# The first block of a two-block transformer layer, turned to token-major like the second

## What is computed

```python
h = rms_norm(x, norm_mix[l])
proj = jnp.einsum('btd,dn->btn', h, w_in[l])
q_a, f_a, i_a, g_a, q_b, k_b, v_b, gate_logits = jnp.split(proj, split_pts, axis=-1)
gates = jax.nn.sigmoid((gate_logits + b_gate[l]).astype(jnp.float32)).astype(x.dtype)
gate_a, gate_b = jnp.split(gates, 2, axis=-1)

y_a = hgrn2_mixer(q_a, f_a, i_a, g_a, lower_bounds[l], hgrn_out_gain[l])
y_b = chunked_relpos_attention(q_b, k_b, v_b, q_gain[l], k_gain[l], rel_bias[l])

merged = (gate_a * jnp.einsum('btc,cd->btd', y_a, w_proj_a[l])
          + gate_b * jnp.einsum('btc,cd->btd', y_b, w_proj_b[l]))
x = x + jnp.einsum('btd,de->bte', merged, w_out[l])
```

## Time and profile before

| | |
|---|---|
| median of 3 runs | 2746.28 us (2742.32 to 2750.71) |
| the profiled execution | 2749.1 us, its span 2747.2 us, so 1.9 us lie around the span |
| granted TensorE clock, mean | 0.986 |
| busy: PE matmuls, PE weight loads, DVE, ACT | 97%, 84%, 65%, 45% |
| chain of work that ended last | PE 90%, DVE 4%, DMA 2%, ACT 2% |
| first matmul of group 0 starts | 22.27 us |
| group 15 starts, proj_b ends | about 398 us, about 704 us |

### The profile page before, as it was taken

How to read it: one execution, slowest core, us unless ns; L and a number is a source line. 1 busy time by engine, 2 the same in 40 slices (tenths; PEclk the granted TensorE clock), 3 DMA queues, 4 the chain that set the end, 5 groups by cost and what they waited for, 6 DMA issues and landing times.

```text
span 2747.2 us, 39546 instructions
## 1 busy us (share of the span) xinstructions
PE 2666.8 (97%) x14450; PEld 2318.1 (84%) x14450; DVE 1782.5 (65%) x2072; ACT 1223.1 (45%) x1456; POOL 11.6 (0%) x15
## 2 busy tenths in 40 slices
PE   6999999999999999999999899999879999999998
PEld 6999999999887888888888788887768888888886
DVE  6766653545776777777777676885666565656565
ACT  4444444454454444444444544455444443444343
POOL 0000000000000000000000000000000000000000
PEclk9999998999999999999999999999989999999999
DMA  6865554455788777777777577773646666666663
GB/s 215 262 209 165 154 169 122 150 190 182 241 268 259 251 252 251 248 250 250 253 250 247 156 231 217 214 222 132 209 136 228 209 209 220 208 212 209 209 217 133
DMA packets 304408, 577.52 MB, mean 210 GB/s; under 512 B 17584, under 2 KB 27968, under 8 KB 304016
## 3 DMA queue, kind: packets, MB, share of 16 engines
q1 hardware_dynamic: 303392, 571.58, 65.6%
q0 software_dynamic: 880, 4.02, 0.5%
HBM read 573.42 MB, written 2.11 MB: 209 GB/s over the span
## 4 chain that ended last, share of the span: by engine, by line
PE 90%; DVE 4%; DMA 2%; ACT 2%; issue 2%; SPq 0%; DVEq 0%; ACTq 0%
PE acc L1086 82%; PE W L1086 6%; DMA raw<-in_w_out 1%; PE W L1149 1%; DVE wlo L1525 1%; DMA raw<-in_w_ffn_in 1%; DVE adaacc L1547 1%; ACT whi L510 1%; ACT arena L546 0%; PE W L1255 0%; DVE hL L1586 0%; PE acc L1375 0%; DMA arena<-in_xT 0%; DVE arena L1622 0%; DVE arena L2119 0%
## 5 line engine op out<-in xcount | busy, mean ns | idle before, releaser
L1525 DVE TENSOR_TENSOR wlo<-raw,whi 128x1024 fp32r<-128x1024 f32 x888 | 1080.9, 1224 | 803.6 <-ACT whi L510 800.9
L510 ACT ACTIVATE whi<-raw 128x1024 fp32r<-128x1024 f32 x888 | 935.2, 1059 | 1218.8 <-PE acc L1086 1013.0
L1086 PE MATMUL acc<-whi,hH 128*128 128x512 f32 x1952 | 533.8, 395 | 9.3 <-issue 6.4
L1086 PE MATMUL acc<-whi,hL 128*128 128x512 f32 x1952 | 523.4, 390 | 0.0
L1086 PE MATMUL acc<-wlo,hH 128*128 128x512 f32 x1952 | 522.8, 390 | 0.0
L1086 PEld LDWEIGHTS acc<-whi,hL 128*128 128x128 f32 x1952 | 367.0, 188 | 77.9
L1086 PEld LDWEIGHTS acc<-wlo,hH 128*128 128x128 f32 x1952 | 366.9, 188 | 77.2
L1086 PEld LDWEIGHTS acc<-whi,hH 128*128 128x128 f32 x1952 | 361.9, 189 | 81.1 <-issue 10.6
L1547 DVE SCALAR_TENSOR_TENSOR adaacc<-raw,cs,adaacc 128x512 f32<-128x512 f32 x360 | 269.8, 749 | 8.7 <-DMA raw<-in_w_ada 1.9
L1086 PE MATMUL acc<-whi,yH 128*128 128x512 f32 x864 | 235.6, 395 | 4.8 <-issue 4.8
L1086 PE MATMUL acc<-wlo,yH 128*128 128x512 f32 x864 | 232.1, 391 | 0.0
(11 more groups left out here) (197 smaller groups left out, 1465.3 us busy)
## 6 DMA issues: line engine op xcount, KB each, us to landing
raw<-in_w_in SPq DMA_DIRECT2D x264, 512.0 KB, 4.4
raw<-in_w_ada SPq DMA_DIRECT2D x192, 512.0 KB, 4.7
raw<-in_w_ffn_in SPq DMA_DIRECT2D x176, 512.0 KB, 4.6
raw<-in_w_up SPq DMA_DIRECT2D x128, 512.0 KB, 4.5
raw<-in_w_down SPq DMA_DIRECT2D x128, 512.0 KB, 4.2
raw<-in_w_ffn_out SPq DMA_DIRECT2D x88, 512.0 KB, 4.7
raw<-in_w_out SPq DMA_DIRECT2D x32, 512.0 KB, 4.8
raw<-in_w_o SPq DMA_DIRECT2D x32, 512.0 KB, 4.5
```

What stands on the lines that cost most here:

```text
L510: act.activation(whi[:, v], raw[:, s], ACT.Copy).then_inc(S("w_hi"), 1)
L1086: return pe.matmul(o, l, r, start=start, stop=stop, skip_group_check=True)
L1525: dve.tensor_tensor(wlo[:, v], raw[:, s], whi[:, v].bitcast(F32), ALU.subtract)\
```

## The change

Mode A is gone. All groups of the first block run in mode B, so results have tokens on partitions, and:

- **First norm.** `hH` and `hL` are made from x times the gain alone (`x_low` on DVE). x is loaded a second time by rows; ACT squares it with a running sum behind group 0 (`first_norm`), and rstd, now one number per partition, is a scale of each evacuation (`evac_sig`, `evac_copy`, `silu`, `gate_lin`).
- **f and q** are turned on PE after evacuation (`fq_turn`, 8 transposes each, four times) into the half of `acc` they came from.
- **Head norms**: DVE sums along the free dimension (`head_reduce`), multiplies by the reciprocal roots there, and PE turns the result (`head_turn`, 16 transposes each, three times). `head_sum` and `head_spread` are gone.
- **Gate bias** is a row now: loaded broadcast by the GpSimd queue (`gate_bias`, 8 loads of 256 KB), added on DVE (`gate_lin`), then ACT's sigmoid in place.
- **Merged activations** are turned (`turn_merged`, 8 transposes, four times) before they are split.

```diff
+            sp.dma_start(col[:], A["cols"]).then_inc(S("cols_in"), 16)
+            x_chunk(0)
+            first(0)
+            first(1)
...
+            first(5)
             sp.dma_start(cst[:], A["consts"]).then_inc(S("tables_in"), 16)
+            sp.dma_start(xn0, A["x"].rearrange("(t p) n -> p t n", p=P)).then_inc(S("x_rows"), 16)
+            first(6)
+            first(7)
...
+            for u in range(8):
+                if u % 2 == 0:
+                    act.wait_ge(S(f"x_in{u // 2}"), 16)
+                for j in (2 * u, 2 * u + 1):
+                    ins = act.activation(hH[:, j], x0[:, j], ACT.Identity, scale=V("norm_mix", 1, j))
+                ins.then_inc(S("x_hi"), 1)
                 hi()
...
+                act.wait_ge(S("x_rows"), 16)
+                for t in range(TT):
+                    act.activation(blk(6 + t), xn0[:, t], ACT.Square, accum_out=tot[:, t:t + 1]).then_inc(S("x_sq"), 1)
...
+            group(hooks={2: off_copy, 4: gate_sig(0, M), 5: head_square(0), 7: head_root(0)})
+            group(hooks={0: head_square(1), 1: head_root(1), 2: ya_hi, 3: head_square(2), 4: gate_sig(1, M),
+                         5: head_root(2), 6: head_copy(1)})
+            group(hooks={2: head_copy(2), 4: gate_sig(2, M)})
...
-                            for m in range({"A": GT, "B": 0}[mode]):
-                                ins = mm(a[:, m * T:(m + 1) * T], wt[:, m * P:(m + 1) * P], x[:, kt],
-                                         first and m % 2 == 0, last)
-                            for t in range({"A": 0, "B": TT}[mode]):
+                            for t in range(TT):
                                 ins = mm(a[:, t * GCOL:(t + 1) * GCOL], x[:, kt, t * P:(t + 1) * P], wt, first, last)
...
+            group(8, hH, hL, (), hooks={2: fq_turn(0)})
             pl.phase("q_i")
+            group(8, hH, hL, (("f_in", 1),), hooks={2: fq_turn(1)})
+            group(8, hH, hL, (("f_in", 2),), hooks={3: fq_turn(2)})
+            group(8, hH, hL, (("q_in", 1),), hooks={3: fq_turn(3)})
...
+            group(8, hH, hL, (("vb_in", 2),), hooks={1: hgrn_out, 6: head_turn(0)})
+            group(8, hH, hL, (("gate_lin", 1),), hooks={3: head_turn(1), 6: head_turn(2)})
+            group(8, hH, hL, (("gate_lin", 2),), hooks={7: slot(0, 0, N_B)})
...
+            group(hooks={3: gate_lin(0, M), 6: head_reduce(0), 7: head_apply(0)})
+            group(hooks={1: head_reduce(1), 2: ya_low, 3: gate_lin(1, M), 4: also(head_apply(1), head_reduce(2)),
+                         7: head_apply(2)})
+            group(hooks={3: gate_lin(2, M)})
...
+                hooks = {3: lambda: turn_x1(i - 1)} if i else {1: turn_merged(3)}
```

More of the change, by code:

```diff
@@ L484, in _ @@
             pool.wait_ge(S("ext_out"), 16)
-            pool.wait_ge(S("hn_done"), 1)
+            gate_bias(0)
+            gate_bias(1)
+            for n in (2, 3):
+                pool.wait_ge(S("gate_lin"), n - 1)
+                gate_bias(n)
+            pool.wait_ge(S("hn_in"), 1)
             src = bass.AP(scratch.tensor, 0, [[1, P], [EXT, H], [1, T]])
             pool.dma_start(tiles(HK), src).then_inc(S("hk_in"), 16)
+            for n in range(4, 8):
+                pool.wait_ge(S("gate_lin"), n - 1)
+                gate_bias(n)
             pool.wait_ge(S("att_s"), N_B)
@@ L701, in _, with head_copy @@
-            group(hooks={2: head_root(2), 3: gate_sig(16, 136, mg(2), 8)})
+                act.wait_ge(S("hn_turn"), 1)
+                for h in range(H):
+                    ins = act.activation(yH[:, h], Wf[:, h * T:(h + 1) * T], ACT.Identity, scale=V("out_gain", 1, h))
+                ins.then_inc(S("y_hi"), 1)
+            def head_copy(k):
+                def run():
+                    x, g = ((qb, q_scale[:]), (kb, V("k_gain")))[k - 1]
+                    act.wait_ge(S("hn_turn"), k + 1)
+                    act.activation(x, Wf, ACT.Identity, scale=g).then_inc(S("hn_done"), 1)
+                return run
@@ L745, in _ @@
                 if i:
[L746 removed]
+                    hooks[4] = gate_sig(4 + i - 1, sgb)
                 group(hooks=hooks)
@@ L759, in _ @@
             for i in range(2, 4):
-                group(4, hooks={1: lambda: merged_hi(i - 2)})
+                group(4, hooks={2: lambda: merged_hi(i - 2)})
             pl.phase("out")
+            hi()
             hi()
@@ L768, in _ @@
             merged_hi(3)
-            for _ in range(4):
+            for _ in range(3):
                 hi()
@@ L1086, in mm, with group @@
                 return pe.matmul(o, l, r, start=start, stop=stop, skip_group_check=True)
-            def group(units, xh, xl, free, mode="A", k0=0, ready=None, hooks={}):
+            def group(units, xh, xl, free, k0=0, ready=None, hooks={}):
                 for name, value in free:
@@ L1748, in decayed, with also @@
                 return run
-            group(begin=4, hooks={6: bounds})
-            group(hooks={1: edges, 2: masks, 5: forget(0)})
+            def also(*fs):
+                return lambda: [f() for f in fs]
+            group(hooks={0: first_rstd, 1: also(bounds, edges), 2: masks, 5: forget(0)})
             pl.phase("q_i")
             group(hooks={5: forget(1)})
-            group(hooks={5: silu_q(0)})
-            group(hooks={5: silu_q(1)})
+            group(hooks={4: silu_q(0)})
+            group(hooks={4: silu_q(1)})
             group(hooks={3: scan})
@@ L1787, in y_low, with gate_lin, run @@
                 dve.tensor_tensor(yL[:], tiles(src), yH[:].bitcast(F32), ALU.subtract).then_inc(S("y_lo"), 1)
-            def also(*fs):
-                return lambda: [f() for f in fs]
-            group()
-            group(hooks={0: head_rec(0), 3: head_apply(0), 5: also(lambda: y_low(1, ob), head_rec(1))})
-            group(hooks={0: head_apply(1), 2: head_rec(2), 5: head_apply(2)})
+            def gate_lin(n, dst):
+                def run():
+                    g = PHASES["gate_a"][1] + n if n < 4 else PHASES["gate_b"][1] + n - 4
+                    v = PHASES["gate_a"][0] + 8 * (n + 1) if n < 4 else PHASES["gate_b"][0] + 8 * (n - 3)
+                    dve.wait_ge(S("w_used"), v)
+                    dve.wait_ge(S(f"bias_in{n % 2}"), 16 * (n // 2 + 1))
+                    if n == 0:
+                        dve.wait_ge(S("c_done"), 8)
+                    for t in range(TT):
+                        ins = dve.scalar_tensor_tensor(out=cols(dst, n % 4)[:, t], in0=tokens(acc[:, g % 2])[:, t],
+                                                       scalar=rs[:, 0, t:t + 1], in1=brow[:, n % 2],
+                                                       op0=ALU.mult, op1=ALU.add)
+                    ins.then_inc(S("gate_lin"), 1)
+                return run
+            group(hooks={3: gate_lin(0, M), 6: head_reduce(0), 7: head_apply(0)})
+            group(hooks={1: head_reduce(1), 2: ya_low, 3: gate_lin(1, M), 4: also(head_apply(1), head_reduce(2)),
+                         7: head_apply(2)})
+            group(hooks={3: gate_lin(2, M)})
             def att(n, n0, n1):
```

420 lines of the change are left out of this document (212 added, 208 removed).

## The result

The changed kernel took 2709.38 us (median of 4 runs, 2706.16 to 2712.45) where the kernel before took 2745.95 (4 runs, 2742.32 to 2750.71): a ratio of 0.9871, 95% interval 0.9854 to 0.9889. That is 36.6 us less; the forecast was 41 less. The profiled execution took 2709.32 us, with a span of 2707.5 against 2747.2, so 39.7 less on the time line.

A forecast was written before the change was run, and what follows sets the result against it. The prediction took PE, busy 97% of the span, to bound the kernel. Its seven terms summed to -41.0 us, so 2746.3 - 41.0 = 2705 us, with a range of 2690 to 2725.

The forecast's parts named there:

- 1 units: From group 1 on, 168 units go from mode A to B, 0.154 us less each: -25.9 us.
- 2 sums, spreads, clock: Head norms: three sums and three spreads removed, 23.4 us, and the slow clock behind them, 5.7: -29.1 us.
- 3 turns, 13: Added f/q, head and merged turns on PE, 0.9 us per 8 transposes, 1.8 per head turn: +11.7 us.
- 4 start: Group 1 starts at 39.4 us instead of 48.1, less one 2.0 us restart at half clock: -6.7 us.
- 5 head norms: Groups 15 and 16: PE waits ahead of head turns, +4.2, and a fall of the clock, +2.0: +6.2 us.
- 6 levels: PE waits 0.9 us ahead of the levels in groups 7 and 8: +1.8 us.
- 7 loads, groups 2 to 5: Extra loads share the ring with `w_ada` and DVE waits for PE's turns: +1.0 us, between 0 and 3.
- turn in `out`: Last merged turn, behind unit 1 of `out`: costed at nothing, since SP's ring is as slow as PE there.
- (a): Rival: the start has no stall, up to 9 us more gained, 2696 us; chance 0.14.
- (b): Rival: each turn lets the clock fall, 2.0 us each at 13 visible turns, 2729 us; chance 0.09.
- (c): Rival: mode conversion gives nothing because DVE, ACT and the ring are as slow as PE, 2731 us; chance 0.06.
- (d): Rival: slower than before, ring runs empty at each turn, 11 waits of 6.7 us, 2779 us; chance 0.04.

The follow-up runs named there:

- run 1: Changed kernel with 168 units put back to mode A (weights stationary, 256-column matmuls instead of 512): 2727.24 us median, ratio 0.9936 to the kernel before.
- run 2: Kernel before, with the 48 head-sum matmuls streaming 128 columns instead of 1: 2740.2 us, beside 2743.02 for the kernel before.
- run 5: Changed kernel with units 6 and 7 of group 0 loaded ahead of the tables and of x by rows: 2703.61 us.
- run 3: Changed kernel with every f/q turn and every head turn done twice (80 transposes more): 2713.65 us.
- run 4: Changed kernel with each head turn one unit later on PE: 2702.03 us.
- run 6: Changed kernel with ACT's squares and root spread over group 1, exponential and sigmoid behind unit 5 of group 0: 2701.52 us.
- run 7: Changed kernel with units 6 and 7 loaded earlier and the first norm's ACT pieces spread between units, both start edits together: 2702.19 us.

## Why the prediction was right, point by point

The time fell inside the range, for the reasons given. The change's 2709.4 us stand 4 above the forecast of 2705. On PE's time line:

| term | forecast, us | measured, us | from |
|---|---|---|---|
| 1 units | -25.9 | -25.9 | 21.79 and 23.03 per eight, both in one program by run 1 |
| 2 sums, spreads, clock | -29.1 | -29.1 | groups gone; the clock's part shown by run 2 |
| 3 turns, 13 | +11.7 | +11.3 | 0.87 each |
| 4 start | -6.7 | -4.7 | group 1 at 40.70, 7.4 earlier; 2.7 back in three units (1.6 to 2.8 by kernel) |
| 5 head norms | +6.2 | +4.9 | waits 0.65 + 2.41 + 0; clock 0.65 + 1.18, absent in run 5 |
| 6 levels | +1.8 | +2.5 | waits 1.3; five levels 0.24 longer, 1.2 |
| 7 loads, groups 2 to 5 | +1.0 | +0.2 | from group 1 to the level of group 6 136.05, the parts 135.8 |
| turn in `out` | 0 | +1.8 | 0.87 and a wait of 0.9 |

The measured column sums to -39.0, beside the 39.7 of the spans. Up to `out`'s start the terms sum to -40.8, and the traces show 40.7 (663.64 against 704.35); at the next turn, behind 12 units of `out`, the traces show 38.7 (698.28 against 737.02), where the terms give 39.0. The medians differ by 36.6. The profiled execution of before was 2.8 above the median that the sum was set against, and the median of the change is as its profiled one, so some 3 us of the missing 4 are the spread of the runs and not a term.

**Right.** The place and the kind of each cost: mode B's gain; the end of group 0 set by DMA (unit 7 at 28.5 in the working; unit 6 at 28.29 and the next right behind it); PE idle while ACT squares; the largest wait ahead of `head_turn(1)` (3.1 in the working, 2.41 found); the clock's fall there; no fall behind a turn. The fall is right with some luck: the prediction took it as certain, and run 5 has the same wait without it.

**Mis-sized, term 4.** "I charge one restart at half clock with the 2.0 us of rows 3": it measured 2.7 in the change and in run 1, 2.8 in run 5, 1.9 in run 3 and 1.6 in run 4, behind the same 5.5 us of idling. The half clock itself is there: 0.50 from 40.70 to 44.00 us in the change. And group 1 came at 40.70, not 39.4. ACT's block was as long as reckoned, 8.5 us (31.00 to 39.51) where 29.6 to 38.3 is 8.7, but it began 1.4 later: units 6 and 7 landed together, and ACT rounds both, with x's last piece between them, ahead of the squares. PE ended group 0 at 35.2, not 32.3: the working has one unit left when the last lands, but unit 6 landed no earlier than 28.3 either, behind x by rows, so from 29.49 on PE had two units before it (it had waited 0.55 for the first). That shortened its idle from 7 to 5.5 without moving group 1.

**Wrong, the last turn.** "The last, behind unit 1 of `out`, I cost at nothing ... if the ring has slack it costs 0.9 more and up to 1 us of waiting for `by_gate_b`". The second half held: 0.87 and 0.9. PE runs three units without a stop between the merged turns (661.03 to 669.24), and ends them 0.9 before DVE's product of L1913 is done (670.07). The ring had units ready for PE here, so its slower pace hid nothing: of the 40.7 us gained at `out`'s start 2.0 are gone 12 units later, and PE stands still nowhere else between.

**Not foreseen, in term 6.** Five levels cost 0.24 more each once the units around them are in mode B, and are back at 3.57 in run 1. It was costed at nothing, though the trace of the kernel before shows it, with 3.79 and 3.80 for the levels in the v_b groups. Why it costs that stays open; mode B around it isn't enough, since the level of group 6 stays at 3.57. The waits themselves, which mode B makes, were foreseen (1.8 forecast, 1.3 measured).

**Slightly too dear, terms 5 and 7.** The replay of three engines by durations was 0.7 too long at the second head turn and 0.25 at the first; the turns among the loads of groups 2 to 5 found the ring ready.

Of the rivals, (a) did not happen, and was tested as an edit: runs 6 and 7 make the start without the stall of 5.5 us and gain 8.3 and 9.3 there, where the forecast gave "up to 9". (b) is refuted for turns of 8 and 16 by the change and run 3 (clock 1.00 behind them), (c) by run 1. (d) did not happen: behind the start no new wait of PE is over 2.41 us, where it needed 3.7 at each of eleven places.

## What to carry to other kernels

When a tuned kernel's bound engine gets faster work, count twice: the gain per unit, and what the faster unit uncovers behind every producer that was just in time; here 4.4 of 25.9 us, found at places that one replay by durations names beforehand, and 1.2 for levels that only a look at all of them in the trace before would have given. Ahead of the first product, look at what stands in the evacuating engine's order between two units: small steps that nobody waits for yet (squares, table loads) belong between later units, not in a block ahead of them, where they cost 5.5 us of idling here. The 48 matmuls that stream one column were dearer here than they look, since what was behind them was 5.7 us slower; wide ones in their place were 7.7 us faster in all. And a fall of the clock behind a stop of PE was here a chance and not a fixed price (behind 2.4 us it came in three kernels of four): one trace with it, or without it, is too little to charge it in full or not at all.

## What the hardware showed that I had not expected

- 48 matmuls with one column in three places pulled the granted clock down (0.72 in the earlier trace rows) and cost 5.7 us behind them; with 128 columns in the same places the clock stayed at 1.00 (run 2).
- 32 transposes in a row, 3.7 us, left the clock at 1.00 (run 3). What a stop of PE cost at the start and at the head turns: behind 1.65 us and less three units kept their normal 8.2 (8.64 in mode A) each time; behind 2.4 us, with a head turn following, 1.8 to 1.9 us of slow clock came in three kernels and none in a fourth (run 5); behind 5.5 us, 1.6 to 2.8 came in all five.
- PE's first matmuls ran at about half rate (in run 7 four in 2.05, 1.91 and 1.91 us, where it is 1.07 later; in run 6 2.05, 1.60 and then 1.07), though the stage's granted clock reads 1.00 there (run 7, 9 to 12 us). At the restart of the change the same rate, four in 2.04 us, shows as 0.50. So a clock of 1.00 behind the very first start did not say here that the engine is fast; the duration of a matmul did.
